# A ring of sixteen weight slots instead of twelve, expert loops that take four experts a turn, and seven chunks loaded during the last dense chunks

## The reference

```python
def moe_ffn(h, w_router, b_router, w_gate_up, b_gate_up, w_down, b_down):
    logits = (hf @ w_router).astype(jnp.float32) + b_router.astype(jnp.float32)
    top_v, top_i = lax.top_k(logits, TOP_K)          # 4 of 32 experts for each token
    top_w = jax.nn.softmax(top_v, axis=-1)
...
```

## Time and profile before

| | us |
|---|---|
| median of the runs | 2097.19 |
| the profiled execution | 2101.47 |
| its span, first to last instruction | 2099.7 |
| PE busy | 2066.3 (98%) |
| PE weight loads busy | 1250.5 (60%) |
| DVE, ACT, POOL busy | 860.7, 455.7, 368.3 |
| mean granted TensorE clock | 0.997 of full |
| share of the chain that ended last: PE, DMA | 62%, 16% |

### The profile page before, as it was taken

One profiled execution on the slowest core, in us unless ns is written; L12 is line 12 of the kernel. 1 busy time (PEld: TensorE's weight loads), 2 busy tenths in 40 slices (PEclk: granted clock), 3 DMA queues, 4 the chain that ended last, 5 costly groups with the idle time before them and its releaser, 6 DMA issues.

```text
span 2099.7 us, 42669 instructions
## 1 busy us (share of the span) xinstructions
PE 2066.3 (98%) x17798; PEld 1250.5 (60%) x17798; DVE 860.7 (41%) x1468; ACT 455.7 (22%) x741; POOL 368.3 (18%) x413
## 2 busy tenths in 40 slices
PE   9999998999999999999999999999999999999999
PEld 6888876344344344443343333447786778888887
DVE  4554535432342333333332333324565443444544
ACT  4151442000000000000000000014454532212221
POOL 2010001122232232222222222221201400000000
PEclk9999999999999999999999999999999999999999
DMA  7333114999999999999999999974121021323231
GB/s 261 101 121 130 61 40 170 418 411 406 409 414 407 409 412 410 409 410 411 408 413 406 407 411 401 411 247 140 54 74 41 1 81 61 109 91 100 81 102 58
DMA packets 141108, 520.02 MB, mean 248 GB/s; under 512 B 16460, under 2 KB 71936, under 8 KB 91808
## 3 DMA queue, kind: packets, MB, share of 16 engines
q1 hardware_dynamic: 120384, 495.02, 59.5%
q0 software_dynamic: 20672, 24.26, 4.8%
HBM read 509.09 MB, written 18.88 MB: 251 GB/s over the span
## 4 chain that ended last, share of the span: by engine, by line
PE 62%; DMA 16%; SPq 2%; ACT 1%; DVE 1%; issue 0%; POOL 0%; POOLq 0%; DVEq 0%; ACTq 0%
PE ps L2226 20%; PE ps L2240 10%; DMA ring_a<-in_w_down 10%; PE ps L396 8%; PE ps L398 8%; PE ps L397 8%; DMA ring_a<-in_w_gate_up 5%; SPq L573 2%; PE ps L2034 1%; PE ps L2028 1%; PE ps L2091 1%; PE ps L2054 1%; PE ps L1984 1%; PE ps L2121 1%; PE ps L498 1%
## 5 line engine op out<-in xcount | busy, mean ns | idle before, releaser
L2226 PE MATMUL ps<-ring_a,xe 128*32 128x512 f32 x3912 | 435.8, 593 | 4.5 <-DMA ring_a<-in_w_gate_up 2.7
L2240 PE MATMUL ps<-ring_a,act_t 128*32 128x256 f32 x6000 | 332.8, 379 | 6.8 <-DMA ring_a<-in_w_down 5.7
L2226 PEld LDWEIGHTS ps<-ring_a,xe 128*32 128x32 f32 x3912 | 125.6, 110 | 288.1 <-issue 239.3
L2240 PEld LDWEIGHTS ps<-ring_a,act_t 128*32 128x32 f32 x6000 | 196.8, 110 | 150.2 <-issue 20.4
L2226 PE MATMUL ps<-ring_b,xe 128*32 128x512 f32 x2232 | 247.2, 592 | 0.0
L396 PE MATMUL ps<-xt_hi,hi 128*128 128x512 f32 x544 | 214.1, 394 | 0.8 <-DVE ff_a L1714 0.8
L398 PE MATMUL ps<-xt_hi,lo 128*128 128x512 f32 x544 | 212.2, 390 | 0.0
L397 PE MATMUL ps<-xt_lo,hi 128*128 128x512 f32 x544 | 212.2, 390 | 0.0
L1120 ACT ACTIVATE glu<-glu 128x768 f32<-128x768 f32 x32 | 27.0, 844 | 639.9 <-DVE glu L1667 639.9
L770 POOL DMA_INDIRECT x_rows<-ye,idx x96 | 152.6, 1590 | 38.0 <-issue 38.0
L2226 PEld LDWEIGHTS ps<-ring_b,xe 128*32 128x32 f32 x2232 | 71.0, 110 | 147.1 <-issue 139.6
(11 more groups left out here) (343 smaller groups left out, 2597.4 us busy)
## 6 DMA issues: line engine op xcount, KB each, us to landing
ring_a<-in_w_gate_up SPq DMA_DIRECT2D x163, 1024.0 KB, 25.2
ring_a<-in_w_down SPq DMA_DIRECT2D x125, 1024.0 KB, 27.1
ring_b<-in_w_gate_up SPq DMA_DIRECT2D x93, 1024.0 KB, 26.7
raw<-in_w_in SPq DMA_DIRECT2D x20, 1024.0 KB, 6.6
raw<-in_w_gate SPq DMA_DIRECT2D x11, 1024.0 KB, 5.4
raw<-in_w_up SPq DMA_DIRECT2D x11, 1024.0 KB, 5.4
raw<-in_w_down SPq DMA_DIRECT2D x11, 1024.0 KB, 4.8
raw<-in_w_out SPq DMA_DIRECT2D x8, 1024.0 KB, 5.0
```

The source lines that it names most:

```text
L2226: last = pe.matmul(ps[QUAD * j:QUAD * j + QUAD, g, :], xe[:, g, QUAD * k:QUAD * k + QUAD], w[:, j, :, :], start=k == 0, stop=k == KT - 1)
L2240: last = pe.matmul(y_block(g, j, bank), act_t[:, g, QUAD * (2 * c + h):QUAD * (2 * c + h) + QUAD], w[:, h, QF * j:QF * j + QF], start=c == ...
```

## The change

The ring gets 16 slots in one run of SBUF from 0 to 128 KB per partition. The four new ones are the two halves of `x` (16 KB), the 8 KB of `hbuf`, and one 8 KB gap that the old layout left in `xt_hi`/`xt_lo`'s 32 KB. `m_slot` gives the order in which slots are first filled. Since 12 chunks an expert and 16 slots meet again after 48 chunks, SP's and PE's loops now take four experts a turn (`TURN`), with seven turns and three experts written out behind them; `n_blk`'s second number is now the number of such turns. DVE's, ACT's and POOL's loops stay as they are. Seven chunks of expert 0 are issued ahead of the writes of `h_rows`: three when `raw` slots come free, four when `hi` and `lo` slots do. The first chunks of stream `SB` wait for other slots of the ring. The feed-forward takes its load semaphores from the streams, which frees three for the new slots.

```diff
-RING = 12
+RING = 16
+TURN = 4
...
-        ring_a = at("ring_a", 0, [P, 9, CW])
-        ring_b = at("ring_b", HT, [P, RING - 9, CW])
+        ring = at("ring", 0, [P, RING, CW])
...
+            for q in range(RAW):
+                sp.wait_ge(SA.lo_ready, SA.n - 2 + q)
+                moe_load(sp, 0, q, q)
+            for q in range(3, 7):
+                sp.wait_ge(SA.group_done, SA.first[SA.n - 2 + (q - 3) // 2])
+                moe_load(sp, 0, q, q)
             for t in range(T):
                 sp.wait_ge(n_h, NS["ffn"] + t + 1)
...
-            return ring_a[:, s, :] if s < 9 else ring_b[:, s - 9, :]
+            return ring[:, (2, 0, 1, 5, 8, 3, 6, 4, 7, 11, 12, 13, 14, 9, 10, 15)[s], :]
...
-            for q in range(RAW):
-                moe_load(sp, 0, q, q)
             sp.wait_ge(SA.group_done, SA.first[SA.n])
-            for q in range(RAW, 9):
+            for q in range(7, 9):
                 moe_load(sp, q // KT, q % KT, q)
             sp.wait_ge(r_lgT, T)
-            for q in range(9, RING):
+            for q in range(9, 13):
                 moe_load(sp, 1, q - KT, q)
+            sp.wait_ge(x_set, 16 * T)
+            for q in range(13, 15):
+                moe_load(sp, 1, q - KT, q)
+            for t in range(T):
+                sp.wait_ge(row_tile[t], 32)
+            moe_load(sp, 1, 15 - KT, 15)
             sp.wait_ge(r_table, 1)
...
-            with sp.Fori(0, n2) as i:
...
+            with sp.Fori(0, n4) as a:
+                for b in range(TURN):
...
+                    for s in range(12):
+                        sp.wait_ge(m_used, a * 48 + (12 * b + s + 1))
+                        q = RING + 12 * b + s
+                        if s < 4:
+                            moe_load(sp, e_now, KT + s, q)
+                        else:
+                            moe_load(sp, e_after, s - 4, q)
...
+            for c, q in enumerate((1, 2, 0)):
+                sp.wait_ge(m_used, n4 * 48 + (12 * (TURN - 1) + q - 3))
                 load_chunk(sp, SB, c)
...
-            dve.tensor_scalar(n_blk[:, 1:2], cnt[:, 6:7], float(NE - 2), None, ALU.add).then_inc(r_table, 1)
+            dve.tensor_scalar(n_blk[:, 1:2], cnt[:, 6:7], 1.0 / TURN, float(NE // TURN - 1), ALU.mult, ALU.add).then_inc(r_table, 1)
...
-            with pe.Fori(0, n1) as i:
+            def expert(a, b):
+                i, q0 = a * TURN + b, 8 + 12 * b
+                landed = lambda q: a * 48 + 16 * (q // RING + 1)
                 gate_up_open(i + 1)
                 for j in range(KT):
-                    gate_up_chunk(j, 8 + j, i * 16 + (16 if j < 4 else 32))
+                    gate_up_chunk(j, q0 + j, landed(q0 + j))
...
+            n4 = pe.value_load(n_blk[0:1, 1:2], min_val=NE // TURN - 1, max_val=MAXB // TURN - 1)
+            with pe.Fori(0, n4) as a:
+                for b in range(TURN):
+                    expert(a, b)
+            for b in range(TURN - 1):
+                expert(n4, b)
```

More of the change, by code:

```diff
@@ L351, in program @@
              "out", "out_evacuated"))
-        f_raw = [sem(f"f_raw_loaded{i}") for i in range(RAW)]
+        f_landed = [SB.landed[i] + 16 * len(range(i, SB.n, RAW)) for i in range(RAW)]
         f_hi, f_lo = sem("f_hi_ready"), sem("f_lo_ready")
@@ L584, in moe_loads @@
+            for t in range(T):
+                sp.wait_ge(row_tile[t], 32)
+            moe_load(sp, 1, 15 - KT, 15)
             sp.wait_ge(r_table, 1)
             n1 = sp.value_load(n_blk[0:1, 0:1], min_val=NE - 1, max_val=MAXB - 1)
-            n2 = sp.value_load(n_blk[0:1, 1:2], min_val=NE - 2, max_val=MAXB - 2)
-            with sp.Fori(0, n2) as i:
[L588 to L596, removed]
-                    else:
-                        moe_load(sp, e_after, q - 8, q)
@@ L599, in moe_loads @@
[L599 to L607, removed]
+            n4 = sp.value_load(n_blk[0:1, 1:2], min_val=NE // TURN - 1, max_val=MAXB // TURN - 1)
+            with sp.Fori(0, n4) as a:
+                for b in range(TURN):
+                    e_now = nc.s_assert_within((a * TURN + b) % NE, 0, NE - 1)
+                    e_after = nc.s_assert_within((a * TURN + (b + 2)) % NE, 0, NE - 1)
+                    for s in range(12):
[5 more added lines that the diff above has]
+                            moe_load(sp, e_after, s - 4, q)
@@ new lines, in moe_loads @@
+            for b in range(TURN - 1):
+                for s in range(8 if b == TURN - 2 else 12):
+                    sp.wait_ge(m_used, n4 * 48 + (12 * b + s + 1))
+                    q = RING + 12 * b + s
+                    if s < 4:
+                        moe_load(sp, NE - TURN + b, KT + s, q)
+                    elif b < TURN - 2:
+                        moe_load(sp, NE - TURN + b + 2, s - 4, q)
+                    else:
+                        moe_load(sp, NE - 1, KT + s - 4, q)
@@ L621, in ffn_load @@
                 sp.wait_ge(f_lo, q1 + (q0 - RAW + 2))
-            sp.dma_start(raw3(f_slot(q0), k), src).then_inc(f_raw[q0 % RAW], 16)
+            sp.dma_start(raw3(f_slot(q0), k), src).then_inc(SB.loaded[f_slot(q0)], 16)
         def ffn_loads(sp):
@@ L630, in ffn_loads @@
                 sp.wait_ge(f_lo, j * 3 + 1)
[L631 removed]
+                sp.dma_start(raw3(f_slot(2), KT), dyn(wg, j + 1)).then_inc(SB.loaded[f_slot(2)], 16)
                 ffn_load(sp, dyn(wu, j + 1), KT, 3, j * 3)
@@ L1144, in f_split_hi @@
         def f_split_hi(act, q0, used, count, j=None):
-            act.wait_ge(f_raw[q0 % RAW], (q0 // RAW + 1) * 16 if j is None else j * 16 + (q0 // RAW + 1) * 16)
+            landed = f_landed[f_slot(q0)] + 16 * (q0 // RAW + 1)
+            act.wait_ge(SB.loaded[f_slot(q0)], landed if j is None else j * 16 + landed)
             act.wait_ge(used, count)
@@ L2270, in moe_tensor @@
                 for c in range(4):
-                    down_chunk(c, 16 + c, i * 16 + 32)
+                    down_chunk(c, q0 + 8 + c, landed(q0 + 8 + c))
+            n4 = pe.value_load(n_blk[0:1, 1:2], min_val=NE // TURN - 1, max_val=MAXB // TURN - 1)
+            with pe.Fori(0, n4) as a:
+                for b in range(TURN):
+                    expert(a, b)
+            for b in range(TURN - 1):
+                expert(n4, b)
             pe.wait_ge(m_at, n1 + 1)
             for c in range(4):
-                down_chunk(c, 8 + c, n1 * 16 + 16, 5)
+                down_chunk(c, 44 + c, n4 * 48 + 48, 5)
             pe.wait_ge(rel_dma, 32)
```

## The result

The changed kernel takes 2132.22 us (median of 4, 2131.51 to 2132.78). The kernel before took 2099.19 us beside it (median of 4). The ratio is 1.0157, with a 95% interval of 1.0139 to 1.0174: 33 us slower, where I had forecast 5; the time lies outside my range of 2086 to 2113. The profiled execution has a span of 2129.7 us, 30.0 over the 2099.7 of before.

A forecast was written before the change was run, and what follows sets the result against it. The prediction took the expert stage as bound by weight supply, slightly slower than PE. Six jumps at 3.5 us less 15.9 us of waits gave +5.1 us on 2097.19, say 2102 us; range 2086 to 2113.

The forecast's parts named there:

- The bound and the debt: Expert stage: PE needs 31.24 us an expert, weights about 32.4; landing grows 1.285 us a turn, 15.9 us to gain.
- my two terms, 15.4 and 1.2: Expert stage: excess over 29 turns, 15.4 us, and the last turn's addition, 1.2 us; taken as 15.9 us.
- Early loads: Before the expert stage: seven chunks issued between 281 and 332 us put the DMA engines 18.9 us ahead.
- Part 2: Four more slots in the weight ring: only the last three experts would wait, 3.5 us; about 12.4 us go.
- the allowed time to landing: Expert stage: how long a slot's new chunk may take before PE waits; said to grow from 28.6 to 39.1 us.
- 13 x 16 KB for 48 MB of weights, nothing: Expert stage: DMA traffic of instruction blocks fetched again at the jumps, taken as negligible beside the weights.
- Part 3: PE's loop of four experts: 12.7 code blocks aren't held, so six jumps back each fetch code, 21.0 us in all.
- a stall of 0.9 us an expert: PE's loop of four: jump cost spread per expert, said to let supply catch up and recover the 3.5 us left.
- The size of a jump: PE's jump back: a fetch of 4.4 us less 0.9 us of queue cover, 3.5 us each; this case's chance 0.50.
- The rival of a slow fetch: PE's jumps: fetch takes 6.1 us or more, 5.2 a jump, 2112 us; with 9.7 us fetches 2134; chance 0.23.
- The supply decides: PE's jumps are free because code is held or brought in ahead; time 2085 us; chance 0.13.
- The ring doesn't deliver: Weight ring: early loads late or DMA engines idle longer for want of slots; gain some 10 us; no chance given.

The follow-up runs named there:

- parked chunks: Kernel before plus seven early loads and four added slots holding expert 10's down chunks, its turn written out between two one-expert loops: 2087.72 us, ratio 0.9943.
- pair with a fixed tile: PE multiplies by a fixed tile: sixteen slots, six early loads, loops of two, 2093.44 us (ratio 0.9960); the kernel before, 2101.26 us (1.0001).

## Why the prediction was wrong

- **The bound and the debt: right.** PE at 31.24 us an expert, a debt of 1.285 us a turn, 15.9 us to be had (my two terms, 15.4 and 1.2, add up to 16.6; the account of the result holds with either). With parked chunks the landing time grew from 7.85 us (chunk 36, issued at 448.15) to 18.12 (chunk 132, issued at 697.89): 10.27 us in 8 turns, 1.284 a turn.
- **Early loads: right as a place, wrong as a worth.** They went out at 281 to 332, `h_rows` at 339.71, and the first reuse at 383.58. But "about 4 us of the lead are lost for want of free slots" was too little: 8 to 10 were lost by chunks 30 to 42, and in twelve slots all but 1.7.
- **Part 2, the 12.4 us: about right in size where both kernels have the same code** (7.8 us in the pair with a fixed tile, 12.4 between the written-out kernels of two chips), but the changed kernel can't have it. In it the stalls repay the debt anyway, and with the code written out the blocks cost about what the ring brings (11.4 of 12.4). One term was wrong: the allowed time to landing did not grow from 28.6 to 39.1 us. With sixteen slots and written-out code it stood at 29.2 (median, 1000 to 1300) where before it was 29.0; SP's issues themselves take longer then (see the last section), so a load goes out later than its slot comes free. I had written the blocks off as "13 x 16 KB for 48 MB of weights, nothing"; written out they cost 0.12 us each, 11.4 us for 93. In the changed kernel no such cost is left over in the account by turns.
- **Part 3, that the jumps miss: right.** 146 blocks against the 135 forecast (14.8 a jump and not 13; in the loop of three (155 - 38 - 9) / 9 = 12.0 and not 9.6: about two more than the body for each jump), idle at the first matmul of a turn, no chunk waits, landing far under 30 us. The turns are 132.8 us and not 125 to 129. One sentence of the working was the wrong way round: a stall of 0.9 us an expert, under the debt of 1.2, does not let the supply catch up; it would only have let the debt grow too slowly to be felt. At the measured 7.8 us a jump, 1.95 an expert, the supply does catch up.
- **The size of a jump: the step that failed.** I had "a fetch of 4.4 less a cover of 0.9 = 3.5 us". Measured: a branch of 6.1 us, a cover of 1.36, so 4.85 idle. My value lay between the 2.0 and the 6.1 of the earlier trace rows for no better reason than that. The branch took as long as the higher row, a gather between the weights; whether for the same cause no run shows, as none has a missed jump with idle DMA engines. The rival of a slow fetch had 6.1 and 5.2 a jump, and would have said 2112. Its upper end, 2134, lies 2 us from the result by luck: it had 8.8 us of idle PE for each jump, where 4.85 were measured. What no case had is the 2.95 us behind the jump, where the granted clock has fallen: 7.8 in all. 6 x (7.8 - 3.5) = 25.8 us is the error of the sum (25 of span).
- **The rivals.** "The supply decides" needed the code to be held, and is refuted by the loops of three and four. "The ring doesn't deliver" holds for neither pair of kernels with the same code. It looked so only where sixteen slots with written-out code were set against twelve slots with held code.

## What to carry to other kernels

Before a loop body is lengthened, count its blocks of code on each engine: a body that is held costs 0.2 us a jump, and one that isn't costs here 8 us, so that two jumps eat all that a better supply could give the whole stage (15.9 us). Code that is written out instead has a price as well, here 0.12 us a block beside a saturated weight stream. And where more buffer is to be had but its period would force a longer loop, keep the ring and its loop, and use the added space once, for data loaded ahead while the DMA engines are idle, so that loads are left out in the middle of the saturated stretch.

## What the runs showed of the hardware

- A taken branch of PE to code that isn't held takes 6.1 us (6.6 in the loop of three) with the DMA engines full (share 0.97 about the jump), and 0.2 us where it is held. A body of 6.4 blocks of 16 KB is held and one of 9.6 is not. The Trainium skill (Runtime: NRT & Kernel Launch, Instruction fetch mechanics) has the wait for a fetch at such a branch; its duration is in these rows.
- After 5 us of idle time PE's granted clock has fallen from 1.00 to 0.50 for some us (0.83 over the 20 us about the jump); with 0.34 us idle it stays at 1.00.
- Code fetched in program order stalls PE nowhere from the second to the 21st expert of the written-out kernel with sixteen slots: each takes 31.24 or 31.25 us. But its weight chunks come every 2.744 us and not every 2.709, and in the kernel before 93 more blocks cost 11.4 us.
- SP's issues of 1 MB loads grow longer when many are on the way, with twelve slots as with sixteen. Between 1000 and 1300 the kernel before, the written-out kernel with sixteen slots, and the changed kernel show (ns min/median/max of an issue; below it, us to landing):

```profile
L573 SPq DMA_DIRECT2D ring_b<-in_w_gate_up x28: 333/2417/4572, 1006.1 to 1297.7; - x28
...
DMA to landing us min/median/max: 27.2/29.0/29.8
```

```profile
L579 SPq DMA_DIRECT2D ring<-in_w_gate_up x75: 332/2057/8148, 999.3 to 1299.0; - x75
...
DMA to landing us min/median/max: 27.0/29.2/33.6
```

```profile
L579 SPq DMA_DIRECT2D ring<-in_w_gate_up x73: 332/333/333, 1001.3 to 1298.6; - x73
...
DMA to landing us min/median/max: 4.9/9.6/13.3
```

  An issue takes some 2 us and not 0.33 where the time to landing is near 29 us. At 2.7 us a chunk that is about eleven chunks on the way, an estimate from these rows. With sixteen slots the time to landing hardly grew beyond that; whether still more slots would change it was not tried.
